# A three-layer kernel: six places of its hand-written orders rearranged, and the start of its first layer

## The chip, the cores and the metric

The kernel runs on one core of a Trainium2 chip. The core has a matrix engine (TensorE, PE in the profile), a vector engine (VectorE, DVE), a scalar engine (ScalarE, ACT), a general one (GpSimd, POOL) and a queue engine for transfers (SyncE, SP). Each runs its own list of instructions in order, and they wait for one another through semaphores. The metric is the device time of one execution in microseconds (us), as the median of several runs.

## The reference, cut to what matters

256 tokens of width 1024 pass three layers in fp32, each a mixer and a gated FFN with RMS norms around both. The mixer of layer 0 is RWKV-7, that of layer 1 is MLA attention with 16 heads, and that of layer 2 is an attention branch beside a state-space branch (SSD) over one common input projection.

```python
# layer 0 (rwkv7_time_mix)
rkv = jnp.einsum('nbtd,nde->nbte', xs[:3], w_rkv)
decay = jnp.exp(-jnp.exp(w_log))                 # w_log from tanh(xw @ w1) @ w2
a = jax.nn.sigmoid(a0 + (xa @ a1) @ a2)
kk = (k * k_k).reshape(B, T, H, N)
kk = kk / jnp.maximum(jnp.sqrt(jnp.sum(kk * kk, axis=-1, keepdims=True)), 1e-12)
k = k * (1.0 + (a - 1.0) * k_a)
_, y = lax.scan(_rwkv7_step, S0, seq)            # S = S*w + (S a) b + v k ; y = S r
bonus = (jnp.sum(rh * kh * r_k, axis=-1, keepdims=True) * vh).reshape(B, T, D)
out = ((yn + bonus) * g) @ w_o
# layer 1 (mla_attend), 16 heads, blocks of 128 queries
p = softmax(where(mask, (q_nope k_nope + q_rope k_rope) * scale, -1e30)); o = p v; m = o @ o_w
# layer 2: the two branches, then one output projection
ssd_y = rms_norm((y_fwd + y_bwd + d_skip * xs) * silu(z), ssd_norm)
mixed = (g_attn * attn_out + g_ssd * (ssd_y @ w_ssd_proj)) @ w_out
# after each mixer an FFN, for instance conv_ffn in layers 0 and 1
gate, up = split(x @ w_in); h = gelu(conv(gate)) * up; return h @ w_out
```

## The kernel before

**Tiles and products.** The 256 tokens are two tiles of 128 (a = 0, 1), the width is eight chunks of 128 (c). A product in full precision is made of three matmuls: each operand is split into a high part and a remainder, and `product` issues high times high (L282), high times remainder (L283) and remainder times high (L284). L288 and L289 are a form of it in the FFN output.

**Weights.** All weights stream from device memory through a ring of four slots of 128x2048 values. SP issues the loads (`send`, L3310), a slot at a time, as the products free them. Every slot is split once: ScalarE copies its high part into the arena (`split_act`, L411), VectorE subtracts that from the slot to leave the remainder (`split_dve` through `split_lo`, L417; `split_half`, L428, does half a slot and `split_act_half`, L439, half of the copy). A product with a slot waits for its remainder. `ahead(engine, n, split)` issues the splits up to slot n at that place of the engine's list.

**Orders.** There is no scheduler: the order on each engine is that of the code, and no engine overtakes itself. The functions below are named by engine: `rwkv_pe`, `rwkv_act`, `rwkv_dve`, `rwkv_pool` for the same stage, `mla_*` and `block_*` likewise.

**Front of layer 0.** ScalarE and VectorE mix and split the inputs of the key, value and receptance products (`xs_split_act` L1154, `xs_split_lo` L1160, `mixed` L1710). PE makes the small hidden product of decay and rate, ScalarE copies its two halves out (L1511, L1512), PE multiplies them again (L1217), ScalarE applies eight sigmoids (L1519). Then PE takes the four slots of the key weights (w_k), sums the squared keys by heads, and takes the four slots of w_r. Meanwhile VectorE scans the decays (L1735), clamps the key sums (`key_maxima`, L1742), of which GpSimd takes the power (L1914), and ScalarE spreads them to rows (`key_norms_wide`, L1539), which PE transposes (L1208) between the slots of w_r. The key factor 1 + (a - 1) k_a is made on VectorE: eight operations (L1757) give (a - 1) k_a, one more (L1762) multiplies by it plus one. Later, VectorE inverts small triangular blocks (L1803, L1805), which leave and come back through device memory: SP stores them (L1999, L2005) and loads them rearranged in pieces (`load_z`, L1993) between the loads of w_o, and PE uses what came back (L295). `bonus_sums` sums the bonus of a tile by heads.

**Front of an FFN.** While the second token tile is still being normalized (post scale L518, update L537, mean L554, `x_scaled` L566), PE already multiplies the first tile by two early weight tiles p = 0, 1 (`early`), whose remainders VectorE makes with `early_lo` (L789). `early_turn` (L811) transposes an early result, `xn_turns` (L375) transposes the normalized tokens, whose high part ScalarE copies (L451) and whose remainder VectorE makes (`turn_dve`, L462). `keep_busy` (L389) issues matmuls of the identity with itself whose result is not used.

**MLA.** `squares` (L2273) sums squares of the latents, `kv_weights_hi` (L2294) copies the high part of the key-value weights, and what follows of the latents goes by L2400 on VectorE to L2120 on PE. Per head h, PE forms `scores(h)` (L2165 and L2182), VectorE takes `maxima(h)` (L2483), ScalarE the exponentials `exps(h)` (L2335), PE transposes them (`turn_p`, L2191) and ScalarE evacuates (`evac`, L2344), then PE multiplies by the values (`values`, L295). `roped` (L2478) finishes the rotated part of the queries of a head.

**Layer 2, end of the mixer.** VectorE adds and gates the state-space output (L3227, L3231), normalizes it (`y_variance` L3201, `y_normed` L3235), gates the attention output (`attention_gated`, L3209), splits the slots of the state-space projection, and PE transposes and multiplies (L375, L282).

## Time and profile before

| what | value |
|---|---|
| runs, us | 1084.61, 1084.67, 1086.76 (median 1084.67) |
| profiled execution, us | 1088.07 |
| span of its instructions, us | 1086.3 |
| busy, us | PE 1062.1 (98%), DVE 789.6 (73%), ACT 611.6 (56%), POOL 221.4 (20%) |
| moved by DMA | 183.12 MB, mean 169 GB/s, 16 engines 56% busy |

The span runs from the first to the last instruction of the profiled execution; 1.8 us of its time lie outside. Times in the rows below are counted from the start of the span. A row of a timeline has the start, the busy time, engine, line, operation, out<-in, and in brackets how long the engine was idle before it and what ended that. Merged rows (x8) have the time from the first start to the last end. The PE's ends are modelled and overlap, so what counts on PE are its starts.

### The profile page before, as it was taken

What the parts mean: (1) busy time and instruction counts of PE and PEld (TensorE: products, weight loads), DVE (VectorE), ACT (ScalarE), POOL (GpSimd) and SP (SyncE); (2) the same over time, 40 slices, a digit from 0 to 9 for tenths busy, and PEclk for the clock granted to TensorE, in tenths of its full rate; (3) what the DMA queues carried; (4) which work ended last, traced back from release to release, by engine and by line L of the source; (5) the groups of instructions that cost most, each with busy time, mean ns of one, the idle gap of its engine ahead of it and who ended that gap; (6) DMA issues with size and microseconds to landing.
All of it is one profiled execution on the core that took longest, in us unless ns stands there. A gap on an engine that the chain in (4) does not pass through costs nothing.

```text
span 1086.3 us, 18718 instructions
## 1 busy us (share of the span) xinstructions
PE 1062.1 (98%) x7143; PEld 915.8 (84%) x7143; DVE 789.6 (73%) x1092; ACT 611.6 (56%) x965; POOL 221.4 (20%) x234
## 2 busy tenths in 40 slices
PE   7999999999999999999999999999999999999997
PEld 6997798888888888789888888998777889888886
DVE  7997867878885668778888666688868775566543
ACT  6766376656664576855666454644654455544532
POOL 0125483122220021001222201551100001211200
PEclk9999999999999999999999999999999999999999
DMA  8553172656667476354666574555561654666552
GB/s 247 171 176 119 40 237 76 175 158 191 193 193 266 145 149 175 117 142 132 193 193 180 198 284 122 194 187 184 160 172 45 227 158 129 183 179 189 193 194 78
DMA packets 219748, 183.12 MB, mean 169 GB/s; under 512 B 43265, under 2 KB 197614, under 8 KB 219678
## 3 DMA queue, kind: packets, MB, share of 16 engines
q1 hardware_dynamic: 215710, 171.43, 52.7%
q0 software_dynamic: 3392, 8.66, 2.5%
q10 hardware_dynamic: 576, 2.07, 0.5%
q8 instruction: 48, 0.79, 0.3%
q14 instruction: 22, 0.18, 0.1%
HBM read 179.44 MB, written 2.69 MB: 168 GB/s over the span
## 4 chain that ended last, share of the span: by engine, by line
PE 79%; DVE 12%; DMA 3%; issue 2%; ACT 2%; POOL 1%; SPq 1%; DVEq 0%; POOLq 0%; ACTq 0%
PE bank L288 21%; PE bank L282 13%; PE bank L284 12%; PE bank L283 12%; PE bank L289 10%; DVE ring L417 3%; PE bank L295 2%; PE bank L1252 1%; DVE arena L1710 1%; DVE arena L1805 1%; DVE stat L1803 1%; DMA arena<-in_kv_w_up 1%; PE bank L375 1%; PE bank L2182 1%; SPq L3416 1%
## 5 line engine op out<-in xcount | busy, mean ns | idle before, releaser
L417 DVE TENSOR_TENSOR ring<-ring,arena 128x2048 fp32r<-128x2048 f32 (+1 forms) x138 | 310.3, 2252 | 114.0 <-ACT arena L411 112.4
L282 PE MATMUL bank<-arena 128*128 128x512 f32 (+3 forms) x980 | 343.9, 351 | 2.3 <-DVE ring L417 1.5
L288 PE MATMUL bank<-arena 128*128 128x512 f32 x960 | 335.7, 396 | 0.0
L411 ACT ACTIVATE arena<-ring 128x2048 fp32r<-128x2048 f32 (+1 forms) x145 | 272.3, 1880 | 96.9 <-DMA ring<-in_ffn_w_out 43.3
L289 PE MATMUL bank<-arena,ring 128*128 128x256 f32 x960 | 267.2, 278 | 0.0
L284 PE MATMUL bank<-arena 128*128 128x512 f32 (+3 forms) x720 | 264.8, 368 | 0.0
L283 PE MATMUL bank<-ring,arena 128*128 128x512 f32 (+2 forms) x560 | 216.1, 386 | 0.0
L288 PEld LDWEIGHTS bank<-arena 128*128 128x128 f32 x960 | 180.1, 188 | 42.6
L282 PEld LDWEIGHTS bank<-arena 128*128 128x128 f32 x980 | 185.4, 189 | 27.7 <-issue 4.3
L289 PEld LDWEIGHTS bank<-arena,ring 128*128 128x128 f32 x960 | 180.6, 188 | 0.0
L284 PEld LDWEIGHTS bank<-arena 128*128 128x128 f32 x720 | 135.6, 188 | 22.2
L283 PEld LDWEIGHTS bank<-ring,arena 128*128 128x128 f32 x560 | 105.3, 188 | 20.0
L283 PE MATMUL bank<-arena 128*128 128x256 f32 (+3 forms) x420 | 122.0, 290 | 0.0
L889 ACT ACTIVATE arena<-bank 128x256 f32<-128x256 f32 x60 | 23.1, 385 | 116.5 <-PE bank L289 116.5
L283 PEld LDWEIGHTS bank<-arena 128*128 128x128 f32 x420 | 80.3, 191 | 1.1
L970 POOL CAST arena<-arena 128x256 f32 (+1 forms) x60 | 27.4, 456 | 255.9 <-DVE arena L925 255.9
L284 PE MATMUL bank<-arena,ring 128*128 128x256 f32 x260 | 73.5, 283 | 0.0
L932 DVE TENSOR_TENSOR arena<-bank,arena 128x256 f32<-128x256 f32 x120 | 45.3, 419 | 28.8 <-ACT arena L889 28.7
L529 POOL TENSOR_TENSOR stat<-stat 128x1 f32<-128x1 f32 x12 | 6.7, 555 | 260.6 <-DVE stat L524 260.6
L944 DVE SCALAR_TENSOR_TENSOR arena<-arena,cols 128x255 f32<-128x255 f32 x80 | 50.9, 636 | 9.7 <-ACT arena L895 0.8
L972 POOL TENSOR_TENSOR arena<-arena 128x256 f32 (+1 forms) x60 | 49.3, 822 | 9.6 <-POOL arena L970 8.6
L284 PEld LDWEIGHTS bank<-arena,ring 128*128 128x128 f32 x260 | 49.8, 191 | 0.0
(338 smaller groups left out, 1271.8 us busy)
## 6 DMA issues: line engine op xcount, KB each, us to landing
ring<-in_ffn_w_in SPq DMA_DIRECT2D x80, 512.0 KB, 5.1
ring<-in_ffn_w_out SPq DMA_DIRECT2D x44, 512.0 KB, 4.5
ring<-in_w_gate_up SPq DMA_DIRECT2D x40, 512.0 KB, 5.0
ring<-in_w_in SPq DMA_DIRECT2D x18, 1024.0 KB, 5.0
ring<-in_a_w_rkv SPq DMA_DIRECT2D x12, 1024.0 KB, 5.7
ring<-in_w_down SPq DMA_DIRECT2D x22, 512.0 KB, 3.7
ring<-in_a_w_o SPq DMA_DIRECT2D x4, 1024.0 KB, 7.9
arena<-in_ffn_w_in SPq DMA_DIRECT2D x8, 512.0 KB, 5.0
```

The costliest lines, as they stand in the source:

```text
L282: nc.tensor.matmul(dst, stationary[0], moving[0], start=start, stop=False)
L283: nc.tensor.matmul(dst, stationary[0], moving[1], start=False, stop=False)
L284: return nc.tensor.matmul(dst, stationary[1], moving[0], start=False, stop=stop)
L288: nc.tensor.matmul(dst[:, :], stationary[0], both_parts, start=start, stop=False)
L289: return nc.tensor.matmul(dst[:, 0:T], stationary[1], hi, start=False, stop=stop)
L411: nc.scalar.activation(buf(hi_of(n), 0, w, arena12), ring[:, r, 0:w], ACT.Copy).then_inc(hi_ready, 1)
L417: on.tensor_tensor(ring12[:, r, 0:w], ring[:, r, 0:w], buf(hi_of(n), 0, w, arena12).bitcast(F32), ALU.subtract).then_inc(split_ready, 1)
L889: nc.scalar.activation(whole_sum[0][j % 2], bank[pair][:, T:2 * T], ACT.Copy).then_inc(act_done, 1)
L932: nc.vector.tensor_tensor(whole_sum[g][j % 2], bank[pair + g][:, 0:T], whole_sum[g][j % 2], ALU.add).then_inc(conv_step, 1)
L944: nc.vector.scalar_tensor_tensor(conv[:, back:T], gate[:, 0:T - back], conv_at(f, it, j, tap[i]), conv[:, back:T], ALU.mult, ALU.add).then ...
L970: nc.gpsimd.tensor_copy(tile_cells(fT_hi, it, j), gated[seat(j)]).then_inc(ffn_hi, 1)
L972: nc.gpsimd.tensor_tensor(tile_cells(fT_lo, it, j), gated[seat(j)], tile_cells(fT_hi, it, j).bitcast(F32), ALU.subtract).then_inc(ffn_done, 1)
```

## The change

1. **FFN fronts.** In all three FFNs PE transposes the second token tile before it turns the early results, and the `keep_busy(pe, 4, 2)` is gone. In the first FFN `early_lo(0, 0)` moves from the start of `ffn_front_dve` to between the last two operations `o_lo` of `rwkv_dve`, and `early_lo(0, 1)` takes its place, so that none stands between `turn_dve` and `post_scale(1)`.
2. **Front of layer 0.** On ScalarE the second half of the key's input split moves behind the two hidden copies. The eight operations of the key factor go from VectorE to ScalarE, as copies with scale k_a and bias 1 - k_a (`Identity`), behind the second split of w_r; VectorE computes the bias once and then multiplies plainly. On VectorE the last split of w_k goes ahead of the scans, `key_maxima(0)` and the first split of w_r into their middle, `key_maxima(1)` ahead of the second split of w_r. On ScalarE `key_norms_wide(1)` goes ahead of two of the exponentials. The last split of w_r moves up by one operation.
3. **Bonus sums of tile 1** go from the value product into the second loop of `pairs`, to another bank; their `keep_busy` is gone.
4. **SP** issues the two late groups of `load_z` each ahead of a load of w_o, where each stood behind one.
5. **MLA.** On ScalarE `squares(1, 1)` moves ahead of `kv_weights_hi(1)`. In the heads' loop PE goes head by head where it went by pairs, ScalarE and VectorE likewise, and the halves of the o_w splits move up.
6. **Layer 2.** On VectorE the first half split of the state-space projection moves behind the first gating, `y_gated(1)` behind `attention_gated(0)`, and the second half split, `y_variance(1)` and the first `turn_dve` ahead of `y_normed(1)`.

The diff, cut:

```diff
             if f != 1:
-                early_lo(dve, f, 0 if f == 0 else 1)
+                early_lo(dve, f, 1)
             turn_dve(dve, turn, 0, 4, hi, lo)
-            if f == 0:
-                early_lo(dve, f, 1)
...
             early(0, 0)
             early(1, 0)
+            xn_turns(pe, i - 1, 1)
             early_turn(0, 0)
-            xn_turns(pe, i - 1, 1)
             early_turn(1, 0)
-            keep_busy(pe, 4, 2)
             early(0, 1)
...
             def bonus_sums(a):
                 pe.wait_ge(bonus_ready, 1)
...
-                    mm = by_columns(bank[6][:, a * H + 2 * c:a * H + 2 * c + 2],
+                    mm = by_columns(bank[(6, 0)[a]][:, a * H + 2 * c:a * H + 2 * c + 2],
...
-                if s == 2:
-                    pe.wait_ge(tok_evac, 4)
-                    bonus_sums(1)
-
...
             for l in range(PAIR_BANKS):
+                if l == 4:
+                    pe.wait_ge(v_evac, 1)
+                    bonus_sums(1)
...
             xs_split_act(act, "k", 0)
-            xs_split_act(act, "k", 1)
             after_slots(act, "lora_wa")
             nc.scalar.activation(lora[0:64, 0:T], bank[3][0:64, 0:T], ACT.Tanh).then_inc(lora_hidden, 1)
             nc.scalar.activation(lora[64:P, 0:T], bank[3][64:P, 0:T], ACT.Copy).then_inc(lora_hidden, 1)
+            xs_split_act(act, "k", 1)
...
             ahead(act, FIRST["w_r"], split_act)
             keys_out(2)
             ahead(act, FIRST["w_r"] + 1, split_act)
+            act.wait_ge(kk_ready, 1)
+            for c in range(DC):
+                op = nc.scalar.activation(chan(W_T1)[:, c, :], chan(W_A)[:, c, :], ACT.Identity, scale=col("a_k_a", c),
+                                          bias=key_bias[:, c:c + 1])
+            op.then_inc(iclr_sig, 1)
             keys_out(3)
             key_squares(1)
             key_norms_wide(0)
...
             nc.scalar.activation(buf(W_EM), buf(W_CUM), ACT.Exp, scale=KAPPA).then_inc(decay_exp, 1)
+            key_norms_wide(1)
             nc.scalar.activation(buf(W_SIG), buf(W_SIG), ACT.Exp, scale=-KAPPA).then_inc(decay_exp, 1)
             nc.scalar.activation(s_scale, last_e, ACT.Exp, scale=-KAPPA).then_inc(decay_exp, 1)
-            key_norms_wide(1)
...
+            ahead(dve, FIRST["w_k"] + 2, split_dve)
             mixed("g")
-            ahead(dve, FIRST["w_k"] + 2, split_dve)
             mixed("v")
+            nc.vector.tensor_scalar(key_bias, cols[:, COL["a_k_a"]:COL["a_k_a"] + DC], -1.0, 1.0, ALU.mult,
+                                    ALU.add).then_inc(kk_ready, 1)
...
+            ahead(dve, LAST["w_k"], split_dve)
             dve.wait_ge(decay_sig, 4)
             for c in range(DC):
                 for a in range(NT):
                     t = slice(a * P, (a + 1) * P)
                     op = nc.vector.tensor_tensor_scan(cum[:, c, t], const("ones"), sig[:, c, t], 0.0, ALU.mult, ALU.add)
                 if c == 3:
-                    ahead(dve, LAST["w_k"], split_dve)
+                    key_maxima(0)
+                    ahead(dve, FIRST["w_r"], split_dve)
             link(dve, op)
...
-            key_maxima(0)
-            ahead(dve, FIRST["w_r"], split_dve)
...
             nc.vector.tensor_tensor(buf(W_SIG), buf(W_CUM), buf(W_SIG), ALU.subtract).then_inc(cum_ready, 1)
+            key_maxima(1)
             ahead(dve, FIRST["w_r"] + 1, split_dve)

-            dve.wait_ge(mix_done, MIXED["v"])
-            dve.wait_ge(iclr_sig, 4)
-            for c in range(DC):
-                op = nc.vector.tensor_scalar(chan(W_T1)[:, c, :], aT[:, c, :], 1.0, col("a_k_a", c), ALU.subtract, ALU.mult)
-            link(dve, op)
-            key_maxima(1)
+            dve.wait_ge(iclr_sig, 5)
...
-            k_new = step(nc.vector.scalar_tensor_tensor(buf(W_K), buf(W_T1), 1.0, buf(W_K), ALU.add, ALU.mult))
+            k_new = step(nc.vector.tensor_tensor(buf(W_K), buf(W_T1), buf(W_K), ALU.mult))
             ahead(dve, FIRST["w_r"] + 2, split_dve)
-            dve.wait_ge(decay_exp, 4)
             for hf in range(2):
...
+                if hf == 0:
+                    dve.wait_ge(decay_exp, 4)
                 link(dve, nc.vector.tensor_tensor(buf(W_ADD)[:, at], buf(W_A)[:, at], buf(W_EM)[:, at], ALU.mult))
+                if hf == 0:
+                    ahead(dve, LAST["w_r"], split_dve)
                 nc.vector.scalar_tensor_tensor(buf(W_REMOVE)[:, at], buf(W_KK)[:, at], -1.0, buf(W_SIG)[:, at],
                                                ALU.mult, ALU.mult).then_inc(removal_ready, 1)
-                if hf == 0:
-                    ahead(dve, LAST["w_r"], split_dve)
...
             o_lo(1, 0)
+            early_lo(dve, 0, 0)
             o_lo(1, 1)
...
-            for h in range(4, H, 2):
-                for x in range(2):
-                    turn_p(h + x)
-                    if h + 2 < H:
-                        scores(h + 2 + x)
-                for x in range(2):
-                    values(h - 2 + x)
-                if h == 4:
+            for h in range(4, H):
+                turn_p(h)
+                if h + 2 < H:
+                    scores(h + 2)
+                if h == 6:
                     swapped(3)
-                if h == 12:
+                values(h - 2)
...
+            squares(1, 1)
             kv_weights_hi(1)
-            squares(1, 1)
...
+            o_w = FIRST["o_w"]
+            split_act_half(act, o_w, 0)
             exps(1)
-            o_w = FIRST["o_w"]
             q_rotary(2)
             evac(0)
-            split_act_half(act, o_w, 0)
+            split_act_half(act, o_w, 1)
             exps(2)
             q_even(3)
             evac(1)
-            split_act_half(act, o_w, 1)
+            split_act_half(act, o_w + 1, 0)
...
-            for h in range(4, H - 2, 2):
+            for h in range(4, H - 2):
                 evac(h)
-                if h == 6:
+                if h == 12:
                     split_act_half(act, o_w + 1, 1)
-                evac(h + 1)
                 exps(h + 2)
-                exps(h + 3)
...
+            y_gated(0, y_summed(0))
+            split_half(dve, FIRST["ssd_proj"], 0)
+            y_variance(0)
+            second_sum = y_summed(1)
             dve.wait_ge(yg_gain_landed, 16)
             y_normed(0)
             attention_gated(0)
-            y_variance(1)
+            y_gated(1, second_sum)
             split_half(dve, FIRST["ssd_proj"], 1)
             emitted[dve] = FIRST["ssd_proj"] + 1
+            y_variance(1)
+            turn_dve(dve, TURN_SSD, 0, 0, B_SQ, B_SQ_LO)
             y_normed(1)
-            turn_dve(dve, TURN_SSD, 0, 0, B_SQ, B_SQ_LO)
             attention_gated(1)
...
             rwkv_inverse_sp(sp)
+            rwkv_inverse_late_sp(sp, 0)
             rows_of("w_o", A["a_w_o"][0], 2, range(0, 1))
-            rwkv_inverse_late_sp(sp, 0)
+            rwkv_inverse_late_sp(sp, 1)
             rows_of("w_o", A["a_w_o"][0], 2, range(1, 2))
-            rwkv_inverse_late_sp(sp, 1)
```

VectorE in the front of layer 0, from the third split of w_k (before) or the last split of w_k (after) to the key's multiplication. L417 is a split of a weight slot, L1735 (L1746 after) the scans, L1742 (L1738) the key maxima, L1749 to L1751 the centred sums of decay. Before:

```order
L417 TENSOR_TENSOR ring<-ring,arena 128x2048
L1735 SCALAR_TENSOR_TENSOR arena<-cst,arena 128x128 x8
L1742 TENSOR_SCALAR stat<-bank 128x16
L417 TENSOR_TENSOR ring<-ring,arena 128x2048
L1748 COPY stat<-arena 128x16
L1749 TENSOR_TENSOR arena<-arena,stat 128x2048
L1750 TENSOR_TENSOR stat<-arena,stat 128x8
L1751 TENSOR_TENSOR arena<-arena 128x2048
L417 TENSOR_TENSOR ring<-ring,arena 128x2048
L1757 TENSOR_SCALAR arena<-arena,cols 128x256 x8
L1742 TENSOR_SCALAR stat<-bank 128x16
L1762 SCALAR_TENSOR_TENSOR arena<-arena 128x2048
```

After:

```order
L417 TENSOR_TENSOR ring<-ring,arena 128x2048
L1746 SCALAR_TENSOR_TENSOR arena<-cst,arena 128x128 x8
L1738 TENSOR_SCALAR stat<-bank 128x16
L417 TENSOR_TENSOR ring<-ring,arena 128x2048
L1746 SCALAR_TENSOR_TENSOR arena<-cst,arena 128x128 x8
L1753 COPY stat<-arena 128x16
L1754 TENSOR_TENSOR arena<-arena,stat 128x2048
L1755 TENSOR_TENSOR stat<-arena,stat 128x8
L1756 TENSOR_TENSOR arena<-arena 128x2048
L1738 TENSOR_SCALAR stat<-bank 128x16
L417 TENSOR_TENSOR ring<-ring,arena 128x2048
L1763 TENSOR_TENSOR arena<-arena 128x2048
```

The first L417 is the last split of w_k; before it stood between the scans. The first split of w_r now stands there. The eight L1757 are gone, and the second L1742 (L1738) is ahead of the last L417 of the piece, the second split of w_r.

SP around the inverse blocks, in the scan of layer 0; `y_blocks` is their place in device memory, `in_a_w_o` the output weights. Before:

```order
L1999 DMA y_blocks<-arena 128x1024
L1993 DMA arena<-y_blocks 32x16x32 x8
L2005 DMA y_blocks<-arena 128x1024
L3310 DMA ring<-in_a_w_o 128x2x1024
L1993 DMA arena<-y_blocks 32x16x32 x4
L3310 DMA ring<-in_a_w_o 128x2x1024
L1993 DMA arena<-y_blocks 32x16x32 x4
L3310 DMA ring<-in_a_w_o 128x2x1024 x2
```

After:

```order
L3319 DMA ring<-in_a_w_rkv 128x2x1024 x2
L2002 DMA y_blocks<-arena 128x1024
L1996 DMA arena<-y_blocks 32x16x32 x8
L2008 DMA y_blocks<-arena 128x1024
L1996 DMA arena<-y_blocks 32x16x32 x4
L3319 DMA ring<-in_a_w_o 128x2x1024
L1996 DMA arena<-y_blocks 32x16x32 x4
L3319 DMA ring<-in_a_w_o 128x2x1024 x3
```

Each late group of four loads from `y_blocks` now stands ahead of the load of `in_a_w_o` that it stood behind.

VectorE at the end of the mixer of layer 2, where L428 is a half split of the state-space projection and L417 a full one. Before:

```order
L428 TENSOR_TENSOR ring<-ring,arena 128x1024
L3227 TENSOR_TENSOR arena<-bank,arena 128x512 x2
L3231 TENSOR_TENSOR arena<-arena 128x1024
L3227 TENSOR_TENSOR arena<-bank,arena 128x512 x2
L3201 TENSOR_SCALAR arena<-arena 128x1
L3231 TENSOR_TENSOR arena<-arena 128x1024
L3235 SCALAR_TENSOR_TENSOR arena<-arena 128x1024
L3209 TENSOR_TENSOR arena<-bank,arena 128x512 x2
L3201 TENSOR_SCALAR arena<-arena 128x1
L428 TENSOR_TENSOR ring<-ring,arena 128x1024
L3235 SCALAR_TENSOR_TENSOR arena<-arena 128x1024
L462 TENSOR_TENSOR arena<-bank,arena 128x4x128 x2
```

After:

```order
L3230 TENSOR_TENSOR arena<-bank,arena 128x512 x2
L3235 TENSOR_TENSOR arena<-arena 128x1024
L428 TENSOR_TENSOR ring<-ring,arena 128x1024
L3204 TENSOR_SCALAR arena<-arena 128x1
L3230 TENSOR_TENSOR arena<-bank,arena 128x512 x2
L3239 SCALAR_TENSOR_TENSOR arena<-arena 128x1024
L3212 TENSOR_TENSOR arena<-bank,arena 128x512 x2
L3235 TENSOR_TENSOR arena<-arena 128x1024
L428 TENSOR_TENSOR ring<-ring,arena 128x1024
L3204 TENSOR_SCALAR arena<-arena 128x1
L462 TENSOR_TENSOR arena<-bank,arena 128x4x128 x2
L3239 SCALAR_TENSOR_TENSOR arena<-arena 128x1024
```

The first half split is behind one L3230/L3235 pair (L3227/L3231 before), the second L3235 is behind L3212 (L3209 before), and L462 is ahead of the second L3239 (L3235 before).

## Rows read from the trace of the kernel before

**Rows 1.** Waits of PE: engine, line, what for, us in total, times, longest.

```profile
PE bank L1252 <- ACT arena L1621: 1.8, 1, 1.8
...
PE bank L282 <- DVE ring L417: 1.5, 3, 0.8
...
PE bank L1217 <- ACT arena L1512: 1.4, 1, 1.4
...
PE bank L295 <- DMA arena<-y_blocks: 1.0, 1, 1.0
...
PE bank L375 <- DVE arena L566: 0.9, 1, 0.9
...
PE bank L2165 <- DVE arena L2478: 0.9, 1, 0.9
...
PE bank L2120 <- DVE arena L2400: 0.8, 1, 0.8
...
PE bank L2191 <- ACT arena L2335: 0.8, 2, 0.5
...
PE bank L375 <- DVE arena L3209: 0.7, 1, 0.7
...
PE bank L1208 <- ACT arena L1539: 0.7, 1, 0.7
```

**Rows 2.** The page's chain of work that ended last, by engine.

```profile
PE 79%; DVE 12%; DMA 3%; issue 2%; ACT 2%; POOL 1%; SPq 1%; DVEq 0%; POOLq 0%; ACTq 0%
```

**Rows 3.** Timeline of ACT in the front of layer 0.

```profile
17.75 2.22 ACT L1154 ACTIVATE arena<-arena 128x1024 fp32r<-128x1024 f32 x2
...
30.31 3.06 ACT L1519 ACTIVATE arena<-bank,cols 128x256 f32<-128x256 f32 x8
...
50.49 0.60 ACT L1526 ACTIVATE arena<-bank 128x512 f32<-128x512 f32 x1 [4.85 <-PE bank L284]
...
63.62 1.06 ACT L1539 ACTIVATE arena<-stat 128x1024 f32<-128x1024 f32 x1 [0.97 <-POOL stat L1914]
```

**Rows 4.** Timeline of DVE in the front of layer 0.

```profile
54.03 2.29 DVE L417 TENSOR_TENSOR ring<-ring,arena 128x2048 fp32r<-128x2048 f32 x1
...
56.23 2.18 DVE L1757 TENSOR_SCALAR arena<-arena,cols 128x256 f32<-128x256 f32 x8
```

**Rows 5.** Timeline of PE in the front of layer 0.

```profile
58.05 0.36 PE L282 MATMUL bank<-arena 128*128 128x256 f32 x1
...
65.58 0.36 PE L282 MATMUL bank<-arena 128*128 128x256 f32 x1
```

**Rows 6.** Timeline of POOL in the front of layer 0.

```profile
58.70 4.88 POOL L1914 TENSOR_TENSOR stat<-stat 128x16 f32<-128x16 f32 x1 [6.66 <-DVE stat L1742]
```

**Rows 7.** The chain in order of time around the inverse blocks: start, us, what.

```profile
136.04 6.35 DMA y_blocks<-arena
...
143.87 5.24 DMA arena<-y_blocks
```

**Rows 8.** DMA issues: out<-in, queue, operation, count, KB each, median us to landing.

```profile
ring<-in_a_w_o SPq DMA_DIRECT2D x4, 1024.0 KB, 7.9
...
y_blocks<-arena SPq DMA_DIRECT2D x2, 512.0 KB, 4.5
```

**Rows 9.** Timeline of DVE in the front of the first FFN.

```profile
198.71 2.28 DVE L789 TENSOR_TENSOR arena<-arena 128x2048 fp32r<-128x2048 f32 x1
...
205.42 1.42 DVE L566 SCALAR_TENSOR_TENSOR arena<-x_sb,stat,gpre 128x512 f32<-128x512 f32 x2 [0.66 <-POOL stat L559]
```

**Rows 10.** The chain in order of time at the MLA latents.

```profile
394.18 9.42 DMA arena<-in_kv_w_up
```

**Rows 11.** Timeline of DVE at the end of layer 2's mixer.

```profile
846.13 2.28 DVE L417 TENSOR_TENSOR ring<-ring,arena 128x2048 fp32r<-128x2048 f32 x1
```

**Rows 12.** Timeline of PE, identity matmuls: at the start, and in the second FFN front.

```profile
4.41 2.93 PE L389 MATMUL bank<-cst 128*128 128x128 f32 x12 [4.41 <-DMA cst<-constants]
...
490.49 1.06 PE L389 MATMUL bank<-cst 128*128 128x128 f32 x8
```

89 lines of the change are left out of this document (46 added, 43 removed).

## The prediction

> **What bounds the kernel now.** I read the chain of work that ended last first, then PE's waits, then the timelines around each place that the change touches. The chain is PE for 79% and VectorE for 12% [rows 2], and PE is busy nearly all of the span. So matmuls that stay can't give anything back, and the change takes none away but identity matmuls. What it can win is the time in which PE stands still. PE's own waits in the places that are touched are listed in [rows 1]: ten lines that hold 11.5 us (1.8 + 1.5 + 1.4 + 1.0 + 0.9 + 0.9 + 0.8 + 0.8 + 0.7 + 0.7, read in any order). A gain much above 10 us has no source; the question is which waits really end sooner. The profiled execution took 1088.07 us, 3.4 above the median of the runs (1084.67). I sum differences against the profiled one and take them off the median.
>
> **Front of layer 0, -1.6 (from -2.4 to -1.0).** Three waits of PE lie ahead of the receptance product. The hidden copies come sooner by one half of the key's input split, 1.1 us (two take 2.22 [rows 3]); PE's second hidden product, which waits 1.4 for them [rows 1], can start about 0.5 sooner, since then its own predecessor is late. Two of the three waits for remainders (L282 on L417, 1.5 in all three [rows 1]) are those for the third and fourth slot of w_k, whose splits move ahead of mixing and scans; with the restart after each they are worth about 1.0. So PE would come to the second slot of w_r 1.5 sooner than at 58.05 [rows 5]. VectorE doesn't let it: it is busy without a break here, and the split of that slot ends at 54.03 + 2.29 = 56.32 [rows 4]; ahead of it the change puts a key maximum (0.17) and the bias (0.2), and the input remainder of the receptance comes 0.5 later, since ScalarE's half split is now behind the copies. It ends at 57.2, PE starts at 57.3, and 0.75 is left.
> The other half comes at the second key-norm transpose. PE waits 0.7 for L1539 [rows 1], this for GpSimd's power (0.97 [rows 3]), and that starts at 58.70 and takes 4.88 [rows 6], since the maximum stands behind the eight key factors (56.23, 2.18 [rows 4]). Now the maximum is at 54.9, the power ends at 60.0, the rows are spread by 61.1, and PE, which reaches the transpose at 63.1, does not wait. The third slot starts at 64.0 for 65.58 [rows 5]: -1.6. If VectorE's delay is smaller the end is -2.4, if it costs another 0.6 it is -1.0. From there to the inverse blocks I let it pass on whole, since the masked blocks that VectorE inverts come from PE's products.
> The eight key factors on ScalarE are costed at nothing: eight sigmoids of that shape take 3.06 [rows 3], and ScalarE stood idle for 4.85 before 50.49 [rows 3], just there. Without that cover they would cost up to 3.06. The bonus sums are costed at nothing too: PE waits 1.8 at L1252 [rows 1] for the pairs, which end with VectorE's inverse, and the sums' 1.6 us go into or out of that wait.
> By the Trainium skill (ScalarE: Activation LUTs, What ACT_TABLE_LOAD costs) an operand read by a pointer lengthens an activation, by some 93 ns each; the copies have two and the sigmoids one. By it the eight would take an estimated 3.9, which the idle time still covers, with key squares 0.6 later; no row here shows such a copy.
>
> **SP, -1.0 (from -1.1 to 0, and more below under the rivals).** PE waits 1.0 for the late blocks [rows 1]. They landed 5.24 after 143.87, and could only be asked for after the second store, which took 6.35 from 136.04 [rows 7]; beside it ran the load of the first w_o slot, 1024 KB, 7.9 to its landing [rows 8]. The two stores have a median of 4.5 [rows 8], so the first, with no load beside it, took 2 x 4.5 - 6.35 = 2.65. With w_o behind the blocks the second should end 2 to 3 us sooner, and the blocks by as much. The whole wait goes. Next late is the first w_o slot itself: issued near 141, beside only small pieces, it would land near 148, which is about when ScalarE wants it.
>
> **First FFN's front, -1.55 (from -1.6 to -0.8).** PE waits 0.9 for `x_scaled(1)` (L566) [rows 1], at 205.42 [rows 9]. In front of that chain stands `early_lo(0, 1)` at 198.71 for 2.28 [rows 9], so that the first operation of the second tile waits until 200.9, and its input is there about a microsecond sooner. The chain comes 1.5 sooner. Behind it hang the transpose, both parts of the turn, and PE's next weight tile, which all come sooner by the same 1.5: the input's 1.0 and half a microsecond by which the operations of the first tile's statistics no longer queue behind it. The moved `early_lo(0, 0)` goes to where VectorE waits for ScalarE ahead of its last `o_lo` for longer than the 2.28, and costs nothing; if it doesn't fit there, half is lost and -0.8 is left.
>
> **The other two fronts, -0.2 (from -0.3 to 0).** Eight identity records, 1.06 us each time [rows 12], go. PE's next tile waits for VectorE's turn anyway, so they filled a wait, and only the transpose's earlier place gives 0.1 each.
>
> **MLA latents, -1.0 (from -1.4 to -0.5).** ScalarE does the squares behind the high part of the key-value weights, which waits until these land at 394.18 + 9.42 = 403.60 [rows 10]. The squares' input is there before. Ahead of the weights they come 1.9 sooner, and PE's wait of 0.8 at L2120 [rows 1] goes with its restart. Next late is ScalarE with the query weights.
>
> **Heads of the attention, -0.9 (from -2.0 to +0.5).** The first heads hold waits of 0.9 at L2165 for the rotated queries and 0.8 at L2191 for the exponentials [rows 1]; both are requests in pairs that single heads serve sooner. With restarts some 2 us stand there. Behind the first heads PE is full and head by head costs it no work. I take half. The other end is one wait more of the longest kind of L2191, 0.5.
>
> **End of layer 2's mixer, +0.55 (from -0.5 to +1.0).** The half split (half of a full one's 2.28 [rows 11]) leaves the path to the first normalized tile, and the turn, for which PE waits 0.7 at L375 on L3209 [rows 1], comes 0.8 sooner. But the same product then needs the full split that runs at 846.13 for 2.28 [rows 11]. In front of it VectorE now has the second gating late, so that the second normalization waits on a longer detour over ScalarE and GpSimd; I count it ready at 849.0 for 848.4. What PE won before it is waited away there, and 0.55 is lost.
>
> Sum: -1.6 - 1.0 - 1.55 - 0.2 - 1.0 - 0.9 + 0.55 = -5.7. The profiled execution would take 1082.4, the median is 1079.0.
>
> **Rivals.** *VectorE absorbs it.* In the front of layer 0, in the latents and in layer 2 an engine without slack stands behind the wait that ends. If only the smaller half arrives (0.75, 0.5 at the blocks, 1.2 in the FFN, 0.5 at the latents, nothing at the heads, 0.55 lost) the gain is 2.4: 1082.3. For it: VectorE's chain share of 12% [rows 2]. Against: GpSimd's power, which alone gives 0.8, is clearly early.
> *The store is slow by itself.* If the 6.35 [rows 7] comes from the store's own small pieces, the blocks land no sooner, and the w_o slot, issued near 144, lands 7.9 later [rows 8], near 152 and almost 4 after it is wanted, 2.5 of it seen by PE. Sum -5.7 + 1.0 + 2.5 = -2.2: 1082.5. Against it: the first store, alone, took 2.65.
> *Head by head is worse.* If the tighter interleaving makes PE wait a little at each of the later heads (0.1 for each of 12, and nothing saved at the start), -5.7 + 0.9 + 1.2 = -3.6: 1081.1.
> *The clock falls, and the kernel is slower.* The identity matmuls keep PE's activity up where it waits. At the start of the kernel, after 4.4 us without work, twelve of them took 2.93, 0.24 each; eight in the second FFN's front took 1.06, 0.13 each [rows 12]: half the pace, that of 1.2 and not of 2.4 GHz. If PE falls to it in the idle time of 0.5 to 1 us now left bare, an early tile of 48 matmuls at 0.12 takes 5.8 more. In all three fronts that is 17.3: 1096.3; in one only, 1084.8, no change. The point from which it decides is whether 1 us of idle, once in a front, is enough. Against it: PE stands still for 1.8 us at L1252 [rows 1], and goes on at full pace with the granted clock at 1.00.
> The Trainium skill (TensorE: Matmul & The Clock Gate, the section on the HAM clock gate) has this rule, that TensorE drops to half its clock when it has been idle and wins it back by work. By that rule alone the three fronts would be at risk; the wait at L1252 speaks against it at this length.
>
> **How the numbers follow.** Forecast 0.60 at 1079.0; VectorE absorbs 0.14 at 1082.3; slow store 0.09 at 1082.5; worse heads 0.09 at 1081.1; clock 0.08 (0.05 in all three fronts, 0.03 in one). What a measurement of this kernel can tell from no change is 0.2%, 2.2 us: faster is below 1082.5, slower above 1086.8. Of the forecast nearly all is faster (0.57), of the absorbing case half (0.08), of the slow store half (0.05), of the heads all but a little (0.08): 0.78. Slower is the clock in three fronts and a rest of added misses: 0.07. The rest is 0.15. The forecast's own ends add up to -9.1 and -0.9, which don't come together; two thirds of the way gives -8.0 and -2.5. With the absorbing and slow-store cases the range reaches up to 1083.5, and below to 1075.5, for terms sized too small.
>
> **What would show it.** Right: no wait of PE at L1208 and a GpSimd power from about 55; a third w_r slot at about 64; the second store in under 4 us and no wait of L295 on the blocks; the next tile in the first FFN at 1.5 less than its place; no wait at L2120. In layer 2 a wait of PE on L417 of about a microsecond. Wrong: a new wait of L282 on L417 at w_r above 1 us, a wait on the first w_o slot on ScalarE, waits at L295 or L2191 in most heads, or matmuls of 256 columns 0.24 apart behind an FFN front.

## The result, and the profile after

The changed kernel takes 1093.15 us (median of 9 runs, 1091.99 to 1094.20), the kernel before 1086.76 (9 runs, 1084.61 to 1090.17). The ratio is 1.0061 with a 95% interval from 1.0048 to 1.0073: it is 6.4 us slower. The forecast was 1079.0, with a range of 1075.5 to 1083.5, so both the sign and the range are wrong. (It was worked out from the three runs known then, whose median was 1084.67; as a difference it was -5.7 us.) The profiled execution took 1094.20.

The page of the changed kernel: span, TensorE's busy time, and the granted clock in 40 slices.

```profile
span 1092.1 us, 18666 instructions
...
PE 1064.9 (98%) x7117; PEld 916.3 (84%) x7117; DVE 794.1 (73%) x1085; ACT 614.7 (56%) x973; POOL 218.0 (20%) x234
...
PEclk9999899999999999999999999999999999999999
```

One digit of the clock is an 8 where all were 9: the fifth slice, from 109 to 136 us. The waits of PE in the changed kernel, as in [rows 1] (line, what for, total, times, longest):

```profile
PE bank L1250 <- ACT arena L1623: 6.4, 1, 6.4
...
PE bank L282 <- DVE ring L417: 3.6, 4, 1.6
PE bank L282 <- DVE arena L462: 1.2, 3, 0.4
...
PE bank L1451 <- ACT arena L1642: 0.4, 1, 0.4
```

Of the ten waits of [rows 1], which hold 10.5 us, those for the key norms (L1208), the blocks (L295), the latents (L2120) and `x_scaled` (L375 on L566) are gone, and those in the attention heads are down to 0.5. Two have grown. L1250 (L1252 before), PE's wait for the inverse of layer 0, went from 1.8 to 6.4. The waits of L282 for remainders (L417) went from 1.5 to 3.6; of these 1.6 is one slot of w_out that landed late, near 885, and 0.9 one in layer 2, below.

The chain of the changed kernel around that wait, in order of time (start, us, what):

```profile
123.42 0.23 DVE stat L1805
...
123.68 4.54 DVE arena L1807
...
128.24 0.20 DVE stat L1805
...
129.46 2.83 PE bank L1250 x10
```

L1805 and L1807 are VectorE's steps of the inverse (L1803 and L1805 before). The last ones are short, 0.2 to 0.3 us. One of them takes 4.54. GpSimd's timeline says what else ran then:

```profile
120.12 3.56 POOL L1938 MEMSET arena<- 128x2048 f32 x2 [22.27 <-PE bank L284]
123.63 4.50 POOL L1924 TENSOR_TENSOR arena<-arena,cst 128x2048 f32<-128x2048 f32 x1
```

L1924 is the multiply that masks the read matrices with a triangle. It began at 123.63 and ended at 128.13, and VectorE's step, begun 0.05 later, ended at 128.2. In the kernel before the same multiply (L1921) began behind the end of the inverse, which GpSimd's and VectorE's timelines of before show:

```profile
123.02 3.56 POOL L1935 MEMSET arena<- 128x2048 f32 x2 [23.50 <-PE bank L284]
126.54 4.53 POOL L1921 TENSOR_TENSOR arena<-arena,cst 128x2048 f32<-128x2048 f32 x1
```

```profile
125.54 0.19 DVE L1803 TENSOR_TENSOR stat<-arena 128x31 f32<-128x31 f32 x1
125.77 0.19 DVE L1805 TENSOR_TENSOR arena<-arena,stat 128x31 f32<-128x31 f32 x1
```

The inverse ended at 125.96, the multiply began 0.58 later. Ahead of the multiply stand two memsets which GpSimd starts when the value product has freed its last slot ("<-PE bank L284"). The change let the value product end sooner, by 1.7 us from the front and by 1.2 from the bonus sums that left it, so the multiply came 2.9 us sooner. The steps of the inverse came only 1.6 sooner: the two crossed.

What the long wait did to TensorE's clock is seen in the windows: stretch, length, busy time of PE, PEld, DVE, ACT, POOL with the number of instructions, then the granted clock. Before, behind the wait:

```profile
126.70:131.00 4.30, 4.24 (x33) 3.80 (x34) 3.00 (x9) 2.99 (x10) 4.30 (x1) 1.00 0.54 160
```

After, the wait and what follows it:

```profile
122.00:129.30 7.30, 1.05 (x33) 0.97 (x32) 7.03 (x12) 0.46 (x2) 6.13 (x2) 0.64 0.00 0
129.30:134.00 4.70, 4.54 (x21) 4.35 (x23) 2.17 (x7) 2.08 (x7) 0.00 (x0) 0.50 0.54 154
```

Most of the 48 matmuls of L1250 behind the wait ran at a granted clock of 0.50, the level of 1.2 GHz, and together they took 8.45 us for 6.44.

The rest of the account needs one more reading. The table gives how much later (+) or sooner (-) PE starts the same matmul than in the profiled execution of before, each counted from the start of its span, at places named by the time of before; a term of the account is the difference of two lines. The last column is the kernel before itself, profiled again (e8, below): what moves there moves without any edit.

| at | place | after | e1 | e6 | e10 | e12 | e8 |
|---|---|---|---|---|---|---|---|
| 12.2 | first product | 0.09 | 0.05 | 0.06 | -0.08 | 0.50 | 0.09 |
| 65.6 | third slot of w_r | -1.68 | -1.70 | -1.70 | -1.85 | 0.49 | 0.10 |
| 122.9 | ahead of the wait for the inverse | -2.91 | -2.92 | -2.94 | -3.15 | 0.48 | 0.05 |
| 126.8 | behind it | 2.70 | -1.58 | -1.60 | -1.83 | 0.57 | 0.11 |
| 133.2 | behind the pairs | 4.71 | -0.09 | -1.60 | -0.16 | 0.57 | 0.11 |
| 149.2 | the late blocks used | 3.67 | -1.12 | -2.64 | -1.20 | -0.22 | 0.04 |
| 153.0 | next solution step | 4.28 | 0.48 | -0.75 | -1.20 | -0.22 | 0.04 |
| 166.0 | output of the scan | 3.75 | -0.06 | -1.28 | -1.34 | -0.76 | -0.49 |
| 204.0 | first FFN, first early tile | 3.83 | -0.03 | -1.18 | -1.32 | -0.66 | -0.40 |
| 208.5 | its second tile | 2.27 | -1.59 | -2.56 | -2.70 | -0.49 | -0.44 |
| 320 | late in its input products | 4.22 | 0.40 | -2.58 | -2.71 | 1.51 | 1.53 |
| 345 | its output products | 4.35 | 0.50 | -2.58 | -2.71 | 1.61 | 1.66 |
| 425 | latents done | 3.06 | 0.19 | -3.86 | -4.00 | 1.02 | 2.06 |
| 459 | attention heads done | 2.56 | -0.32 | -4.38 | -4.52 | 1.02 | 2.06 |
| 491.5 | second FFN | 2.41 | -0.47 | -4.38 | -4.52 | 1.08 | 2.06 |
| 612 | behind its input products | 4.52 | 1.65 | -4.38 | -2.41 | 3.20 | 2.06 |
| 839 | layer 2, output of the mixer | 4.21 | 1.49 | -3.95 | -2.74 | 2.90 | 2.08 |
| 848.5 | behind the first turned tile | 4.13 | 1.40 | -4.03 | -2.84 | 2.86 | 2.09 |
| 879.5 | output projection | 6.04 | 1.40 | -4.03 | -2.83 | 2.88 | 2.09 |
| 901.4 | third FFN | 5.83 | 1.21 | -4.03 | -2.83 | 2.95 | 2.06 |
| 1080 | end | 5.83 | 1.23 | -6.14 | -4.93 | 2.94 | 2.06 |

Three things in the column of the changed kernel are not in the forecast: +7.6 from 122.9 to 133.2 (the crossing and the clock), about +2 in each of the first two FFNs (215 to 320 and 500 to 612), and +1.9 at 879, where a slot of w_out landed late.

The second needs a correction of what stands ahead: lines 288 and 289 are the matmuls of the FFN's input products, in `tile`, not of its output. One stretch of 60 us of that loop in the kernel before and after; the number behind PE's busy time is that of its matmuls.

```profile
240.00:300.00 60.00, 60.00 (x349) 52.49 (x348) 50.57 (x65) 36.76 (x56) 12.83 (x22) 1.00 0.68 187
...
930.00:990.00 60.00, 60.00 (x341) 52.06 (x340) 35.00 (x44) 31.72 (x44) 12.56 (x22) 1.00 0.65 183
```

```profile
240.00:300.00 60.00, 60.00 (x342) 52.05 (x341) 49.88 (x66) 37.70 (x55) 13.53 (x22) 1.00 0.67 187
...
930.00:990.00 60.00, 60.00 (x342) 52.02 (x341) 35.23 (x44) 31.67 (x44) 12.52 (x22) 1.00 0.66 182
```

PE has no gap in either and the granted clock is 1.00, but 349 matmuls start in one stretch and 342 in the other. Read by their starts, a pair of L288 (512 columns) and L289 (256) takes 347 ns in one and 353 in the other: 231, 113, 232, 118 and again, or 241, 120, 236, 113, 233, 117 and again. Over the 640 matmuls of an FFN's loop this is 2.1 us (a loop of 111.1 or 113.2). The first two FFNs of before had the quick pattern, its third and all three of after the slow one.

### The profile page after: what moved, and what is told of

It is laid out like the page before. It is cut to its first block, busy times and chain, and to the rows that moved or that the text cites. A ratio compares the mean times of both kernels' runs of the same rounds, so it can differ in the third digit from the quotient of the medians.

```text
span 1092.1 us, 18666 instructions
## 1 busy us (share of the span) xinstructions
PE 1064.9 (98%) x7117; PEld 916.3 (84%) x7117; DVE 794.1 (73%) x1085; ACT 614.7 (56%) x973; POOL 218.0 (20%) x234
## 4 chain that ended last, share of the span: by engine, by line
PE 83%; DVE 8%; ACT 4%; DMA 3%; issue 1%; SPq 0%; POOL 0%; DVEq 0%; POOLq 0%; ACTq 0%
PE bank L288 21%; PE bank L282 14%; PE bank L284 13%; PE bank L283 13%; PE bank L289 10%; PE bank L295 2%; DVE ring L417 2%; PE bank L1250 2%; DVE arena L1807 1%; DVE stat L1805 1%; ACT arena L411 1%; PE bank L2185 1%; PE bank L375 1%; DMA ring<-in_w_out 1%; PE bank L2194 1%
## 5 line engine op out<-in xcount | busy, mean ns | idle before, releaser
L417 DVE TENSOR_TENSOR ring<-ring,arena 128x2048 fp32r<-128x2048 f32 (+1 forms) x138 | 311.4, 2260 | 114.5 <-ACT arena L411 112.7
L282 PE MATMUL bank<-arena 128*128 128x512 f32 (+3 forms) x980 | 343.8, 351 | 5.4 <-DVE ring L417 3.6
L288 PE MATMUL bank<-arena 128*128 128x512 f32 x960 | 339.9, 399 | 0.0
L289 PE MATMUL bank<-arena,ring 128*128 128x256 f32 x960 | 269.6, 281 | 0.0
L284 PE MATMUL bank<-arena 128*128 128x512 f32 (+3 forms) x720 | 264.8, 368 | 0.0
L288 PEld LDWEIGHTS bank<-arena 128*128 128x128 f32 x960 | 180.4, 188 | 44.6
L282 PEld LDWEIGHTS bank<-arena 128*128 128x128 f32 x980 | 185.4, 189 | 31.2 <-issue 4.9
L289 PEld LDWEIGHTS bank<-arena,ring 128*128 128x128 f32 x960 | 181.4, 189 | 0.0
L284 PEld LDWEIGHTS bank<-arena 128*128 128x128 f32 x720 | 135.6, 188 | 22.4
L284 PE MATMUL bank<-arena,ring 128*128 128x256 f32 x260 | 73.5, 283 | 0.0
L284 PEld LDWEIGHTS bank<-arena,ring 128*128 128x128 f32 x260 | 49.8, 192 | 0.0
```

Source lines behind the costliest of these rows:

```text
L282: nc.tensor.matmul(dst, stationary[0], moving[0], start=start, stop=False)
L284: return nc.tensor.matmul(dst, stationary[1], moving[0], start=False, stop=stop)
L288: nc.tensor.matmul(dst[:, :], stationary[0], both_parts, start=start, stop=False)
L289: return nc.tensor.matmul(dst[:, 0:T], stationary[1], hi, start=False, stop=stop)
L417: on.tensor_tensor(ring12[:, r, 0:w], ring[:, r, 0:w], buf(hi_of(n), 0, w, arena12).bitcast(F32), ALU.subtract).then_inc(split_ready, 1)
```

## The experiments

Twelve runs follow; one of them is the kernel before again. Ratios are to runs of the kernel before on the same chip at the same time, with 95% intervals.

**GpSimd's multiply held back (e1).** On the changed kernel:

```diff
             pool.wait_ge(prod_evac, PAIR_BANKS)
+            pool.wait_ge(solved, 1)
             read_masked(W_RB[1])
```

> The changed kernel with one more wait: GpSimd starts its masking multiply of the read matrices (4.5 us) only when VectorE's inverse is finished. Theory A (the multiply and VectorE's operations with two inputs from SBUF exclude each other, and the change pulled the multiply 2.9 us forward, into the last steps of the inverse): no VectorE step of the inverse above 0.5 us, the inverse ends at 124.3 where it ended at 128.6, PE waits about 2.1 us less than the 6.4 plus, with the idle below 3 us, no stretch at half clock; 6.2 us faster than the changed kernel, 1087. Rival B (VectorE's 4.5 us step comes from something else, for instance its own semaphore or an instruction that came late): the step stays, and the time with it, 1093.

Measured: 1090.02, ratio 1.0028 (1.0009 to 1.0046); the changed kernel was at 1.0061. GpSimd and the windows of this kernel:

```profile
124.52 4.51 POOL L1924 TENSOR_TENSOR arena<-arena,cst 128x2048 f32<-128x2048 f32 x1 [0.86 <-DVE arena L1807]
```

```profile
124.90:128.00 3.10, 2.82 (x13) 2.73 (x15) 1.52 (x5) 1.48 (x5) 3.10 (x1) 0.50 0.42 169
```

The step that took 4.53 us takes 0.22, PE's wait is 2.1, and the pairs start 4.3 us sooner than in the changed kernel (-1.58 for 2.70 in the table). So the crossing is theory A's, and B falls. The size is 3 us in the medians for 6.2 expected, of which one part is visible: the clock fell here too, to 0.50, though PE waited only 2.1 us; from 126.8 to 133.2 1.5 us are lost again.

**The bonus sums put back (e2), and moved alone (e3).** The first is the changed kernel with the sums of tile 1 between the slots of the value product again, the second the kernel before with that move alone. The main lines of the second's edit (the first undoes them):

```diff
-                if s == 2:
-                    pe.wait_ge(tok_evac, 4)
-                    bonus_sums(1)
...
+                if l == 4:
+                    pe.wait_ge(v_evac, 1)
+                    bonus_sums(1)
```

> The changed kernel with the bonus sums of tile 1 back between the slots of the value product. Theory A: the value product ends 1.3 us later, GpSimd's multiply starts near 124.9, half a microsecond behind the end of the inverse, and is out of its way: as with the GpSimd wait, 1087, but with no margin, so that single executions may fall back. Rival B: no change, 1093. Rival C (the sums' copy and sums in the second loop of pairs are themselves what costs): 1087 too, but with the sums moved and GpSimd waiting it would stay 1093.

> The kernel before with the bonus sums' move alone. Theory A: GpSimd's multiply comes 1.3 us sooner, from 126.5 to about 125.3, while the inverse ends at 126.0: the last two to four steps of the inverse wait for it, 3.9 to 4.3 us, PE idles for over 6 us, then runs at half clock for some microseconds; 5.5 us slower than before. Rival B: as before.

Measured: 1087.27, ratio 0.9997 (0.9979 to 1.0015), for the first, and 1093.34, ratio 1.0045 (1.0022 to 1.0069), for the second. VectorE and GpSimd in the second:

```profile
125.03 0.22 DVE L1802 TENSOR_TENSOR stat<-arena 128x60 f32<-128x60 f32 x1
125.28 4.50 DVE L1804 TENSOR_TENSOR arena<-arena,stat 128x60 f32<-128x60 f32 x1
129.81 0.19 DVE L1802 TENSOR_TENSOR stat<-arena 128x31 f32<-128x31 f32 x1
```

```profile
125.21 4.49 POOL L1920 TENSOR_TENSOR arena<-arena,cst 128x2048 f32<-128x2048 f32 x1
```

A step of 0.22 us becomes one of 4.50 as soon as the multiply comes 1.3 us sooner, in a kernel that is otherwise the one before. In this trace PE starts the pairs 4.3 us later than before and is 6.2 late at 133.2, where the clock has fallen too. That is what the bonus sums' move does, which the prediction had costed at nothing. Rival C falls with e1: there the sums are moved and GpSimd waits, the long step is gone, and the time is 1090.0, not 1093. (e1 and e2 lie 2.8 us apart in the medians, with intervals that just overlap; their traces differ by 1.9 at the end, 0.7 of it from 133 to 153 and 0.9 at and behind a load near 347.)

**The FFN's pattern: whole fronts, and one line.** Between these traces stood the question of the 2 us in each FFN. Five kernels turn on it. First the changed kernel with GpSimd's wait, PE's order as in the change, and the identity matmuls back (e4); then the kernel before with part 1 of the change alone (e5); then the changed kernel with GpSimd's wait and PE's order and identity matmuls as before (e6), and the same without the identity matmuls (e9); last the kernel before with one line moved (e12):

```diff
-            early_turn(0, 0)
             xn_turns(pe, i - 1, 1)
+            early_turn(0, 0)
             early_turn(1, 0)
             keep_busy(pe, 4, 2)
```

> As the first, with the four identity transposes' worth of matmuls back in each FFN front (behind the second early turn). Whether their removal is what made PE's matmuls in the first two FFNs 2% slower to start (346.5 against 353.4 ns for a pair of lines 288 and 289, 1.8 us for each FFN). If it is: 3.6 us faster than without them. If it is only how the profiled execution fell, or set elsewhere: the same within 0.5 us.

> The kernel before with the FFN fronts' part of the change alone (the early remainders' places, the transposes before the early turns, no identity matmuls). In the traces so far the FFN's output loop runs in one of two repeating patterns, 347 or 353 ns for a pair of its matmuls, 2 us for each FFN; with the old fronts three of six FFNs had the quicker one, with the new fronts none of twelve. Theory D (the new order on PE leads into the slower pattern): the first FFN's front 1.5 us sooner, all three FFNs at 353, the median 0 to 2 us slower than before. Theory E (the pattern is drawn anew in each execution, whatever the order): 1.5 us faster than before, and a quick FFN among the three as often as before.

> The changed kernel with GpSimd's wait (which alone gave 1090.0) and with PE's order and identity matmuls of the FFN fronts as before; VectorE's early remainders stay where the change put them. Theory D: a quick FFN in the trace, the median near 1087. Theory E: 1090, as without.

> As the version with GpSimd's wait and PE's old order in the FFN fronts (1084.1, a quick FFN three times in its trace), but without the identity matmuls. Theory D1 (the place of the transposes decides the FFN's pattern): quick FFNs in the trace, 1084.1. Theory D2 (the identity matmuls decide it): none, 1090. The version with the new order and the identities gave 1089.6, so D1 is the likelier.

> The kernel before with one line moved: in the FFN fronts PE transposes the second token tile before it turns the first early result; the identity matmuls and all else stay. No work and no wait is added. Theory D (this order leads into the slower pattern of the output loop, 353 against 347 ns for a pair, which the eight traces with the old order show in 11 of 24 FFNs and the five with the new one in 15 of 15): no quick FFN in the trace, and 2 to 3 us slower than before, with executions that lie closer together. Theory E: as before.

(Two slips in these texts: the loop is the one of the input products, and the old order's traces showed the quick pattern in 13 of 24 FFNs, not 11.)

| kernel | PE's order in the fronts | identity matmuls | us | ratio to before | quick FFNs of its trace |
|---|---|---|---|---|---|
| e1 | new | no | 1090.02 | 1.0028 (1.0009 to 1.0046) | 0 of 3 |
| e4 | new | yes | 1089.61 | 1.0020 (1.0004 to 1.0035) | 0 of 3 |
| e6 | old | yes | 1084.13 | 0.9976 (0.9961 to 0.9991) | 3 of 3 |
| e9 | old | no | 1087.24 | 0.9995 (0.9979 to 1.0011) | 2 of 3 |
| e5, on before | new | no | 1089.00 | 1.0012 (0.9998 to 1.0026) | 0 of 3 |
| e12, on before | new | yes | 1091.62 | 1.0051 (1.0034 to 1.0068) | 0 of 3 |

The windows of e12 and e6, where before had 349:

```profile
240.00:300.00 60.00, 60.00 (x342) 51.99 (x341) 50.13 (x63) 35.86 (x54) 12.16 (x21) 1.00 0.67 186
525.00:585.00 60.00, 60.00 (x342) 52.05 (x341) 49.84 (x64) 35.59 (x54) 12.45 (x20) 1.00 0.66 183
```

```profile
240.00:300.00 60.00, 60.00 (x348) 52.46 (x347) 50.66 (x67) 38.01 (x55) 13.58 (x22) 1.00 0.68 191
...
930.00:990.00 60.00, 60.00 (x348) 52.50 (x347) 36.51 (x44) 31.78 (x44) 12.52 (x22) 1.00 0.68 187
```

With the transposes ahead of the first early turn all 18 FFNs of six traces had the slow pattern (after, e1, e2, e4, e5, e12); with the old order 13 of 24 had the quick one (before, e3, e6 to e11), at least one in each of the eight traces. e12 adds no work and removes none, and costs 5.3 us in the medians, more than the 2 to 3 expected; the pattern explains 3.4 on average (13 of 24 of three times 2.1), and its own trace ends 2.9 behind that of before. The other 2 us or so stay open. Five of its six executions lie within 0.9 us (1090.80 to 1091.68), those of before beside it within 5, as theory D has it. D holds against E, and D1 against D2: the place of the transposes is what counts. For the identity matmuls e6 and e9 leave it open; the medians lie 2.6 us apart relative to before, and the intervals just overlap. Why the order of ten transposes should set the rhythm of a loop that starts some 8 us later isn't settled: it isn't a wait (PE has none in the loop), not the granted clock (1.00), and not the number of matmuls (e4 and e6 have the same).

**The front of layer 0 alone, on the kernel before (e7).** The edit is part 2 of the diff.

> The kernel before with the front of layer 0 alone (part 2 of the change). Theory A: GpSimd's multiply and the end of the inverse both move 1.8 us forward, so they stay 0.6 apart and nothing collides; PE 1.8 us ahead from the receptance product on, 1.8 us faster than before. Theory F (the gain is given back where PE stands idle for the inverse, by the clock's fall): PE ahead by 1.8 until 125, by 0.3 behind it, the time the same.

Measured: 1086.87, ratio 0.9991 (0.9977 to 1.0005). In its trace PE is ahead by 1.62 at the third slot of w_r, by 1.55 behind the inverse and by 1.76 at 153, so theory A holds, F does not, and the clock stayed at 1.00. In the medians it gives 1.0 us with an interval that takes in 1.8 and 0.

**The kernel before again (e8).**

> The kernel before, unchanged, for a second trace. If the wait of 0.8 at the latents (L2120) and the full clock behind the inverse were chance, one or both differ here. Theory E: one to three FFNs at 347.

Measured, one execution: 1090.20. It had the quick pattern in the second FFN only, no wait at the latents, the full clock behind the inverse, and this wait for remainders, larger than the 1.5 of [rows 1]:

```profile
PE bank L282 <- DVE ring L417: 3.2, 4, 1.6
```

Its column, the last in the table, is what chance does: 2.0 in an FFN, 1.8 at a load that lands late (at 347; the changed kernel had one at 879), of which 1.4 fell away again at the latents, and 0.5 at 166.

**SP's order (e10).** e6 with the two late groups of `load_z` behind the loads of w_o again:

```diff
-            rwkv_inverse_late_sp(sp, 0)
             rows_of("w_o", A["a_w_o"][0], 2, range(0, 1))
-            rwkv_inverse_late_sp(sp, 1)
+            rwkv_inverse_late_sp(sp, 0)
             rows_of("w_o", A["a_w_o"][0], 2, range(1, 2))
+            rwkv_inverse_late_sp(sp, 1)
```

> The same version, identities kept, with SP's order as before. Theory G (the second store takes 6 us with or without the w_o load beside it, so the new order only makes the first w_o slot late): the store again near 6 us, the slot landed by about 144.5 where it landed at 149.3, ScalarE's wait of 4.5 for it gone, PE's 1.0 for the blocks back and its 1.7 on L1643 gone: 0.7 faster. Theory H, the prediction's: 1.0 slower.

Measured: 1083.12 (7 runs), ratio 0.9954 (0.9936 to 0.9971) for 0.9976 (0.9961 to 0.9991). In the changed kernel SP's timeline shows the store and what waits for it, and ScalarE's the wait for the slot:

```profile
140.72 0.34 SPq L2008 DMA_DIRECT2D y_blocks<-arena  x1
147.03 1.90 SPq L1996 DMA_DIRECT2D arena<-y_blocks  x4
148.97 0.49 SPq L3319 DMA_DIRECT2D ring<-in_a_w_o  x1
```

```profile
154.71 1.91 ACT L411 ACTIVATE arena<-ring 128x2048 fp32r<-128x2048 f32 x1 [3.19 <-DMA ring<-in_a_w_o]
```

The store is issued at 140.72 and SP's next load waits for its end until 147.03, 6.3 us, as in [rows 7], though no load of w_o runs beside it. Something else does. GpSimd issues two loads about when the store starts, with the old order and the new; its timeline in the changed kernel, and the page's DMA issues:

```profile
139.02 0.60 POOL L1944 DMA_DIRECT2D arena<-in_a_lnx_w  x1
139.62 0.53 POOL L1945 DMA_DIRECT2D arena<-in_a_lnx_b  x1
```

```profile
arena<-in_a_lnx_w POOLq DMA_DIRECT2D x1, 512.0 KB, 4.7
arena<-in_a_lnx_b POOLq DMA_DIRECT2D x1, 512.0 KB, 6.1
```

They land at 143.7 and 145.8, while the store is under way. In every trace these two loads overlap the second store and none overlaps the first, so whether it is slow by itself or for them no run decides; that the load of w_o doesn't make it slow is shown. In e6, with the same order, the cost is seen on PE:

```profile
PE bank L1452 <- ACT arena L1643: 1.7, 1, 1.7
```

In e10 this wait is gone. By the table the new order wins 1.0 at 149.2 and loses 1.9 at 153.0 (e6), the old one wins the same 1.0 here, since PE comes later to blocks that are there, and loses nothing. From 133.2 to 153.0 the traces with the new order move by +0.1 on average (six, -0.5 to +0.9), those with the old one by -0.7 (seven, -1.0 to -0.1). Where the clock had fallen just before, it is 0.0 (five) for -1.0 (three); where it hadn't, +0.9 (e6 alone) for -0.4 (four). So G holds in that the new order loses, at 0.7 to 1.2 us; of the 2.4 between the two ratios the rest lies within the intervals.

**What pays, together (e11).** The changed kernel with the bonus sums, SP's order, and PE's order and identity matmuls of the fronts as before, without GpSimd's wait.

> The parts that the runs have shown to pay: the changed kernel with the bonus sums, SP's order and PE's order and identities of the FFN fronts as before, without GpSimd's wait. By the differences of the stages: front of layer 0 -1.8, first FFN's front -1.4, attention heads -0.5, latents -0.3 to -1.3, layer 2 0: 4 to 5 us faster than before, 1083.

Measured: 1084.72, ratio 0.9973 (0.9959 to 0.9986), 3.7 us faster than before, for 4 to 5 expected; its trace has one quick FFN. e10, which differs by the moved sums and GpSimd's wait, has the lower median. Both beat the kernel before and the changed one; between them the runs don't decide.

## Why the prediction was wrong

**The step that failed first** is the sentence that the bonus sums are costed at nothing. It looked at PE's wait, into which the sums' 1.6 us go (1.2 in the traces), and not at who is released by the end of the value product. That is GpSimd, with two memsets and the multiply. The wait 1.8 at L1252 was read as slack; it was the tail of a chain on VectorE that stood 0.58 us clear of an engine that shares something with it. The cost: +4.3 for the stalled step (126.8, after against e1), and about 2.0 for the clock. GpSimd did not occur in the sum at all but for its power.

The Trainium skill (SBUF — State Buffer, Who interferes with whom; and the part on the two separate sides of SBUF) says that VectorE and GpSimd share a pair of ports, that an operation holds the pair for its whole length, and that a VectorE operation with two inputs from SBUF needs it against a GpSimd operation that reads SBUF. The traces agree here: L1807 with two inputs from SBUF waits for 4.5 us; the operations with an input from a bank (L1816, beside the multiply before) run on; and the memsets, which read nothing, ran beside the steps of the inverse without lengthening one. In one place they don't. GpSimd's power of [rows 6] reads SBUF too and ran from 58.70 to 63.58, and a split of VectorE with two inputs from SBUF, begun 2.0 us into it, took no longer than elsewhere, in the kernel before (and so in e3, e5, e8 and e12):

```profile
60.74 2.31 DVE L417 TENSOR_TENSOR ring<-ring,arena 128x2048 fp32r<-128x2048 f32 x1
```

So this operation on 128x16 elements didn't hold VectorE for its whole length, the multiply on 128x2048 did. The rule spoke against the change, and the prediction didn't bring it up.

**The second** is "only the transpose's earlier place gives 0.1 each" in the FFN fronts, and the same place in the first one. The fronts' own account was right: 1.56 us in the first FFN for 1.55 forecast (204.0 to 208.5), 0.15 in the second and 0.2 in the third for 0.1 each. But the same line sets the pattern of the loop behind. It cost 2.1 in each FFN that would have been quick, and the kernel before is quick in about half of them. PE's order is worth little for it: with VectorE's moves and PE's old order (e6, e9, e10, e11) the first front still gives 1.38 of the 1.56. Nothing in one trace shows this; two stretches of the same loop in the trace of before, 349 matmuls in 60 us and 341 in 60 us, did show that the loop has two paces, and were not looked at.

The other terms:

- *Front of layer 0*, -1.6: -1.77 in the trace, from the first product on. Rows that answer to [rows 3 to 6], from ScalarE, VectorE, GpSimd and PE:

```profile
45.95 4.04 ACT L1557 ACTIVATE arena<-arena,stat,cols 128x256 f32<-128x256 f32 x8
```

```profile
54.81 2.28 DVE L417 TENSOR_TENSOR ring<-ring,arena 128x2048 fp32r<-128x2048 f32 x1
```

```profile
54.98 4.88 POOL L1917 TENSOR_TENSOR stat<-stat 128x16 f32<-128x16 f32 x1 [4.61 <-DVE stat L1738]
```

```profile
57.28 0.36 PE L282 MATMUL bank<-arena 128*128 128x256 f32 x1
```

  The power starts at 54.98 (54.9 to 55 forecast), the split ends at 57.09 (57.2), PE starts the slot at 57.28 (57.3), third slot at 63.9 (64.0). The eight key factors take 4.04 where eight sigmoids give 3.06, within the 4.85 of idle time. The prediction's estimate from the Trainium skill (ScalarE: Activation LUTs, What ACT_TABLE_LOAD costs), 3.9, was the nearer one.
- *SP*, -1.0: +0.7, by the averages above. What failed is the reading that the load of w_o makes the second store slow; the first store's 2.65 is right (2.63). The rival "the store is slow by itself", given 0.09, had the place and the direction right, with w_o late as it says; its reason isn't shown, since GpSimd's two loads run beside the store each time. It put 2.5 us on PE, where the traces lose 0.5 to 1.9 at 153.
- *Latents*, -1.0: the place wins 1.3 in seven of eight traces with the edit (345 to 425) and 0.3 in one; without it the six traces move by -1.5 to +0.4, -0.3 on average. So an estimate of 0.8 is the edit's, from traces that scatter by more than that. The wait of 0.8 in [rows 1] wasn't there in e3, e8 or e12 either, and was 0.2 in e5.
- *Heads*, -0.9: -0.5, in every trace with the edit, and 0.0 in those without.
- *Layer 2*, +0.55: -0.1 (839 to 848.5). The turn comes 0.9 sooner, and the wait for the full split is there as described, just smaller than what was won:

```profile
844.36 1.03 PE L375 MATMUL bank<-cst,arena 128*128 128x128 f32 x8
...
852.59 0.50 PE L282 MATMUL bank<-arena 128*128 128x512 f32 x1 [0.86 <-DVE ring L417]
```

- *The clock*, a rival at 0.08: the mechanism is real and the place was wrong. It was laid at the bare FFN fronts, where PE stands still for 0.4 to 0.8 us and no trace shows a fall; it came at the wait of the inverse. The reason against it, that PE goes on at full pace behind 1.8 us at L1252, doesn't hold in general: e5 waits 2.0 there and loses 1.4 us by 133.2.

Two slips in the prediction's sums change nothing: the ten waits hold 10.5 us, not 11.5, and the terms' own ends add up to -9.3 and -0.8, not -9.1 and -0.9.

In sum, from the traces: -1.8 - 1.6 - 0.8 - 0.5 - 0.4 - 0.1 for the other terms, +0.7 for SP, +4.3 and +2.0 for the crossing, and 3.4 for the patterns: +5.2, beside 6.4 measured. It is no closer than a microsecond or two: where the clock fell, up to 1.0 of its cost comes back at the late blocks, and single loads move traces by 1.8. The range was too narrow because each term was bounded by its own rows, and none by what it releases on an engine outside the sum.

## What to carry to other kernels

Where an edit lets a stage end sooner, list every engine that its end releases, and lay the next operations of each beside what runs then; GpSimd against VectorE first, for here a multiply of 2048 elements that reads SBUF stopped a step with two SBUF inputs until it ended. A wait of the critical engine is not slack if it is the end of a chain on another engine: ask how far that chain is from its neighbours. And before a small difference is explained from two traces, profile the kernel before twice: here a load and a loop's rhythm each moved about 2 us with no edit, and the clock level 1.4 to 1.7 us between kernels whose edits lay elsewhere.
